# One plain iteration instead of two ahead of the block products of two feed-forward layers

## The chip, the cores and the metric

The kernel runs on one core of a Trainium2 chip. The metric is the device time of one execution in microseconds (us). TensorE (PE in the profile) multiplies, VectorE (DVE) and ScalarE (ACT) work element by element, GpSimd (POOL) helps with normalisation, and SyncE (SP) issues the DMAs. The engines run at the same time, each works through its own instructions strictly in their order, and they wait for each other through semaphores. Before the change the time is 2071.54 us (median of three runs, 2071.41 to 2071.98).

## The reference, cut to what matters

A two-layer encoder over 512 tokens of width 1024, all in float32. Each layer is a SwiGLU feed-forward block, a mixer (neighbourhood attention in layer 0, HGRN2 in layer 1) and a second feed-forward block, each followed by a layer norm.

```python
D_MODEL = 1024; SEQ = 512; DEPTH = 2; D_FF = 2816

def _swiglu(h, w_in, w_out):
    a, b = jnp.split(h @ w_in, 2, axis=-1)
    return (jax.nn.silu(a) * b) @ w_out

for i in range(DEPTH):
    mods = (jax.nn.silu(c) @ ada_w[i] + ada_b[i]).reshape(bsz, 9, D_MODEL)
    h = _modulate(x, mods, 0)
    y = _swiglu(h, ffn_w_in[i, 0], ffn_w_out[i, 0])
    x = _layer_norm(ALPHA * x + 0.5 * mods[:, 2, None, :] * y, ln_g[i, 0], ln_b[i, 0], dtype)
    ...                                   # the mixer, with its own layer norm
    h = _modulate(x, mods, 2)
    y = _swiglu(h, ffn_w_in[i, 1], ffn_w_out[i, 1])
    x = _layer_norm(ALPHA * x + 0.5 * mods[:, 8, None, :] * y, ln_g[i, 2], ln_b[i, 2], dtype)
```

There are four such feed-forward blocks, numbered 0 to 3 here. `h @ w_in` has 22 column tiles of 128 for `a` and 22 for `b`; tile n of `a` and tile n of `b` form pair n.

## The kernel before

**Precision.** Every float32 operand of a matmul is split in two: a rounded high part (`h_hi`, `w_hi`) and the rest (`h_lo`, `w_lo`). A product is three matmuls: high by high, high by low, low by high. ScalarE makes `w_hi` from the loaded weights in `raw`, VectorE makes `w_lo` as `raw - w_hi`. So each weight tile passes SP (DMA), ACT, DVE and PE in this order.

**Phases.** `plan_phases` lists phases, and `drive` writes the instruction order of ACT and DVE for each. A feed-forward block is done in two halves of 12 and 10 pairs; each half has phases that make the gated values `g` and an `out` phase that multiplies by `w_out`. Blocks 0 and 1 make `g` by plain phases (`kind="in"`). Blocks 2 and 3 (`FAST_FFN`) begin half 0 with a plain phase of `PLAIN_ITERS` iterations of two pairs, and do all other pairs in `fast` phases.

**Plain iteration.** Two pairs, four weight tiles of 128x1024 in four slots (s = 0 to 3). TensorE's `unit` (lines 1841 to 1843) does 8 x 3 matmuls of 512 columns for a slot, 96 for two pairs. In the first plain iteration of half 0 `first_units` (lines 1901 to 1918) does 96 such matmuls in another order, while `h` is still being made. After slots 1 and 3, `finish` has ACT take the SiLU (line 819) and DVE multiply and split the result (lines 1179, 1181, 1183: the gate of a pair).

**Block products.** A fast pair computes its two column tiles by seven products of half size in place of eight: each has 4 x 3 matmuls of 256 columns (lines 1855 to 1857), 84 for a pair. They need sums of blocks of `w` and of `h`. DVE makes the sums of `w` for every pair (`fast_sums`, `fast_last_sum`: lines 1077, 1080, 1086). The four sums of `h` are made once for a block, `hs[0..3]` (lines 1148 to 1156, `combine` steps 0 to 3 on DVE); ACT rounds each to `hs_hi` (line 803) and DVE subtracts, giving `hs_lo` (line 1159, `combine` steps 4 to 7). They read `h_full`, which ACT writes at line 984 for these two blocks.

**Order within a fast pair, on TensorE.** Products 0 and 1 need `h` itself; product 1 ends in a bank of its own. Product 2 waits for the second weights, for `hs_lo` of sums 0 and 1, and for `part_kept`: ACT must first copy product 0 out of its PSUM bank (line 766). Product 3 and 4 need the third weights and `hs_lo` 2. Product 5 needs the fourth weights (`fast_low` 3) and `hs_lo` 3. Product 6 needs the last weights and `part_added` 2: DVE must have taken product 4 out of the bank (line 1131). Before a pair starts, the gate of the pair two places earlier must be done (`pair_free`). Meanwhile ACT and DVE prepare the weights of the next pair (`fast` on each engine), so each of these engines has one fixed order of copies, SiLUs, conversions and sums.

**Loads.** SP issues the loads of the weight tiles (line 633) slot by slot, as soon as DVE has made the `w_lo` of what the slot held.

## Time and profile before

| | us |
|---|---|
| median of the runs | 2071.54 (2071.41 to 2071.98) |
| the profiled execution, its own time | 2069.64 |
| its span | 2067.9 |
| TensorE busy | 2039.0 |
| VectorE busy | 1433.9 |
| ScalarE busy | 881.4 |
| GpSimd busy | 244.6 |

In the span, block 2's `g` of half 0 is made from 1007 to 1134 us, and block 3's from 1703 to 1830 us. The rows below are mostly of block 2. A row of a timeline gives the start and the duration in us, the engine, the line and operation, what is written and read, and in brackets the idle time of the engine just before it and what ended it. The distance from one row's start to the next one's is what an instruction costs in a packed queue; the printed duration is some 0.08 us longer, since instructions overlap at their ends.

### The profile page before, as it was taken

To read this page: it belongs to the slowest core of one execution; us is meant where nothing else is said; L and a number is where in the kernel's file an instruction comes from. 1 tells how busy PE (TensorE), PEld (TensorE's weight loads), DVE (VectorE), ACT (ScalarE), POOL (GpSimd) and SP (SyncE) were. 2 spreads that over 40 slices of the span, in tenths; PEclk is the share of its full clock that TensorE was granted. 3 is DMA by queue.
4 is the path that set the end of the run, shared out by engine and by line. 5 is a ranking of instruction groups with operands and counts; after the bars stand their busy time and mean duration, and the time that the engine had idled before them with its cause. 6 is when DMAs were issued, how large, how long until landed. Compare 5 with 4: busy or idle time off the path is not lost.

```text
span 2067.9 us, 34153 instructions
## 1 busy us (share of the span) xinstructions
PE 2039.0 (99%) x11850; PEld 1741.3 (84%) x11850; DVE 1433.9 (69%) x2232; ACT 881.4 (43%) x1420; POOL 244.6 (12%) x236
## 2 busy tenths in 40 slices
PE   7999999999999999999999999999999999999999
PEld 6888888878888888888899899887888878988997
DVE  6867767655558767767788378577767568855875
ACT  5222222455535222222555256375656535533642
POOL 0000000432104000001300000152111232000002
PEclk9999999999999999999999999999999999999999
DMA  9767764342324767664333333332222122333332
GB/s 321 243 181 214 217 193 135 97 112 81 88 82 147 224 182 233 204 177 137 92 92 102 111 92 91 113 112 82 71 71 75 48 72 72 109 99 97 104 94 77
DMA packets 405405, 265.96 MB, mean 129 GB/s; under 512 B 9390, under 2 KB 366158, under 8 KB 405332
## 3 DMA queue, kind: packets, MB, share of 16 engines
q1 hardware_dynamic: 405332, 265.06, 43.3%
q8 instruction: 37, 0.61, 0.1%
q14 instruction: 36, 0.29, 0.0%
HBM read 262.86 MB, written 2.19 MB: 128 GB/s over the span
## 4 chain that ended last, share of the span: by engine, by line
PE 92%; DVE 3%; ACT 2%; POOL 1%; issue 1%; SPq 1%; DMA 0%; DVEq 0%; POOLq 0%; ACTq 0%
PE ps L1841 21%; PE ps L1843 21%; PE ps L1842 21%; PE ps L1855 6%; PE ps L1857 6%; PE ps L1856 6%; PE ps L1937 1%; PE ps L1912 1%; PE ps L1913 1%; PE ps L2193 1%; PE ps L2140 1%; PE ps L1918 1%; PE ps L2125 1%; PE ps L2114 1%; PE ps L2211 1%
## 5 line engine op out<-in xcount | busy, mean ns | idle before, releaser
L812 ACT ACTIVATE w_hi_all<-raw_all 128x1024 fp32r<-128x1024 f32 (+2 forms) x304 | 286.8, 945 | 739.8 <-PE ps L1843 695.3
L1170 DVE TENSOR_TENSOR w_lo_all<-raw_all,w_hi_all 128x1024 fp32r<-128x1024 f32 (+2 forms) x304 | 332.4, 1095 | 353.4 <-ACT w_hi_all L812 352.9
L1841 PE MATMUL ps<-h_hi,w_hi_all 128*128 128x512 f32 x1104 | 434.5, 394 | 2.1 <-ACT gt_sig L913 1.6
L1843 PE MATMUL ps<-h_hi,w_lo_all 128*128 128x512 f32 x1104 | 430.1, 390 | 0.0
L1842 PE MATMUL ps<-h_lo,w_hi_all 128*128 128x512 f32 x1104 | 429.7, 389 | 0.0
L1841 PE MATMUL ps<-g_hi,w_hi_all 128*128 128x512 f32 x704 | 275.0, 391 | 0.0
L1843 PE MATMUL ps<-g_hi,w_lo_all 128*128 128x512 f32 x704 | 274.0, 389 | 0.0
L1842 PE MATMUL ps<-g_lo,w_hi_all 128*128 128x512 f32 x704 | 273.9, 389 | 0.0
L1841 PEld LDWEIGHTS ps<-h_hi,w_hi_all 128*128 128x128 f32 x1104 | 207.2, 188 | 48.7 <-issue 2.3
L1843 PEld LDWEIGHTS ps<-h_hi,w_lo_all 128*128 128x128 f32 x1104 | 207.2, 188 | 43.9
L1842 PEld LDWEIGHTS ps<-h_lo,w_hi_all 128*128 128x128 f32 x1104 | 207.3, 188 | 41.6
L1700 POOL TENSOR_TENSOR zsum<-zsum,x 128x512 f32<-128x512 f32 x42 | 59.6, 1420 | 1382.2 <-DVE x L1207 1381.3
L1855 PE MATMUL ps<-hs_hi,w_hi_all 128*128 128x256 f32 x576 | 163.0, 283 | 0.0
L1856 PE MATMUL ps<-hs_lo,w_hi_all 128*128 128x256 f32 x576 | 163.0, 283 | 0.0
L1857 PE MATMUL ps<-hs_hi,w_lo_all 128*128 128x256 f32 x576 | 163.0, 283 | 0.0
L1843 PEld LDWEIGHTS ps<-g_hi,w_lo_all 128*128 128x128 f32 x704 | 132.1, 188 | 27.7
L1841 PEld LDWEIGHTS ps<-g_hi,w_hi_all 128*128 128x128 f32 x704 | 132.2, 188 | 27.2
L1842 PEld LDWEIGHTS ps<-g_lo,w_hi_all 128*128 128x128 f32 x704 | 132.2, 188 | 26.9
L1440 DVE SCALAR_TENSOR_TENSOR acc<-ada_all,c_silu,acc 128x512 f32<-128x512 f32 x192 | 143.6, 748 | 5.7
L1855 PE MATMUL ps<-h_hi,w_hi_all 128*128 128x256 f32 x432 | 122.4, 283 | 2.5 <-DVE g L1131 2.5
L1857 PE MATMUL ps<-h_hi,w_lo_all 128*128 128x256 f32 x432 | 122.2, 283 | 0.0
L1856 PE MATMUL ps<-h_lo,w_hi_all 128*128 128x256 f32 x432 | 122.2, 283 | 0.0
(318 smaller groups left out, 3455.4 us busy)
## 6 DMA issues: line engine op xcount, KB each, us to landing
raw_all<-in_ffn_w_in_dram SPq DMA_DIRECT2D x176, 512.0 KB, 3.8
ada_all<-in_ada_w_dram SPq DMA_DIRECT2D x128, 512.0 KB, 4.0
raw_all<-in_ffn_w_out_dram SPq DMA_DIRECT2D x64, 384.0 KB, 3.5
raw_all<-in_ffn_w_out_dram SPq DMA_DIRECT2D x64, 320.0 KB, 3.2
raw_all<-in_hgrn_w_in_dram SPq DMA_DIRECT2D x32, 512.0 KB, 3.7
raw_all<-in_na_w_qkv_dram SPq DMA_DIRECT2D x24, 512.0 KB, 3.8
boot<-in_ada_w_dram SPq DMA_DIRECT2D x8, 512.0 KB, 7.1
boot<-in_ada_w_dram SPq DMA_DIRECT2D x16, 256.0 KB, 6.5
```

The lines of the kernel that those rows point to most:

```text
L812: nc.scalar.activation(w_hi[s][:, 0:ph.kt, :], raw[s][:, 0:ph.kt, :], ACT.Copy).then_inc(S.w_hi_done, 1)
L1170: nc.vector.tensor_tensor(w_lo[s][:, 0:ph.kt, :], raw[s][:, 0:ph.kt, :], w_hi[s][:, 0:ph.kt, :].bitcast(F32), ALU.subtract).then_inc(S.w_l ...
L1440: nc.vector.scalar_tensor_tensor(out=acc[:, 0:width], in0=w, scalar=c_silu[:, row:row + 1], in1=acc[:, 0:width], op0=ALU.mult, op1=ALU.add ...
L1700: nc.gpsimd.tensor_tensor(zsum[:], zsum[:], x[:, bass.ds(tile, 1)], ALU.add).then_inc(S.zsum_done, 1)
L1841: nc.tensor.matmul(ps[:, bank, :], w_hi[s][:, k, :], a, start=start and k == 0, stop=False)
L1842: nc.tensor.matmul(ps[:, bank, :], w_hi[s][:, k, :], b, start=False, stop=False)
L1843: ins = nc.tensor.matmul(ps[:, bank, :], w_lo[s][:, k, :], a, start=False, stop=stop and k == ph.kt - 1)
L1855: nc.tensor.matmul(ps[:, bank, 0:TH], w_hi_all[:, at, :], hi[:, k, :], start=start and k == 0, stop=False, skip_group_check=True)
L1856: nc.tensor.matmul(ps[:, bank, 0:TH], w_hi_all[:, at, :], lo[:, k, :], start=False, stop=False, skip_group_check=True)
L1857: ins = nc.tensor.matmul(ps[:, bank, 0:TH], w_lo_all[:, at, :], hi[:, k, :], start=False, stop=k == KH - 1, skip_group_check=True)
L1912: nc.tensor.matmul(ps[:, bank, :], w_hi[s][:, at, :], h_hi[:, at, :], start=at == 0, stop=False)
L1913: nc.tensor.matmul(ps[:, bank, :], w_lo[s][:, at, :], h_hi[:, at, :], start=False, stop=False)
```

## The change

`PLAIN_ITERS` goes from 2 to 1, so in blocks 2 and 3 the plain phase consists of `first_units` alone, and two more pairs per block, 4 in all, are done by block products: 10 in half 0 and 10 in half 1, 20 of 22. The sums of `h` no longer have a second plain iteration to lie in, and `drive` places them anew: sums 0, 1 and 2 right after the layer norm, ahead of the conversion of the first fast pair's weights; `hs_lo` 0 and 1 after the first gate, sum 3 after the third weights, `hs_lo` 2 ahead of the second gate and `hs_lo` 3 behind it. ACT's `hs_hi` copies move with them. The loops of the plain phase that are now empty are left out.

```diff
@@
-PLAIN_ITERS = 2
+PLAIN_ITERS = 1
@@ def steps(i), in drive
                             finish(ph, i - 1, s)
-                        if ph.combine and isinstance(i, int):
-                            combine(ph, s)
@@
-                elif ph.ada is not None and ph.ada.start == 1 or ph.combine:
+                elif ph.ada is not None and ph.ada.start == 1:
                     steps(1)
                     first = 2
@@
+                if ph.combine:
+                    for c in range(3):
+                        combine(ph, c)
                 for s in range(0 if tail is not None and ph.mixer is not None else max(ph.body, 4)):
+                    if ph.combine and s == 3:
+                        combine(ph, 6)
                     if nxt is not None and s < min(nxt.body, 4) and not (ph.last and s == 3):
                         convert(nxt, 0, s)
                     if s < ph.body:
                         finish(ph, ph.iters - 1, s)
-                    if ph.combine:
-                        combine(ph, 4 + s)
+                    if ph.combine and s == 1:
+                        combine(ph, 4)
+                        combine(ph, 5)
+                    if ph.combine and s == 2:
+                        combine(ph, 3)
...
+                if ph.combine:
+                    combine(ph, 7)
                 end(ph, ph.iters - 1)
@@ SyncE: loads
-                else:
+                elif ph.iters > 1:
                     with sp.Fori(1, ph.iters) as i:
@@ ScalarE: combine
-                for c in [(), (0,), (1,), (2,), (3,), (), (), ()][s]:
+                for c in [(0,), (1,), (2,), (3,), (), (), (), ()][s]:
@@ TensorE
-                    if ph.mixer is None:
+                    if ph.mixer is None and ph.iters > 1:
                         with pe.Fori(1 if peeled else 0, ph.iters - 1 if closing else ph.iters) as i:
                             units(i)
```

**VectorE, first place: from the last `h_lo` of block 2's layer norm on.** `hs` are the sums of `h`, `h_all`, `mean` and `w_t` the sums of a fast pair's weights, `g_0` the first gated pair. Before:

```order
L1511 TENSOR_TENSOR h_lo<-h_full,h_hi 128x512 [waits h32_done] x5
L1170 TENSOR_TENSOR w_lo_all<-raw_all,w_hi_all 128x1024 [waits w_hi_done]
L1148 TENSOR_TENSOR hs<-h_full 128x1024 [waits h32_done]
L1170 TENSOR_TENSOR w_lo_all<-raw_all,w_hi_all 128x1024 [waits w_hi_done]
L1179 TENSOR_TENSOR g_0<-s_tmp,ps 128x512 [waits silu_done]
L1181 TENSOR_SCALAR g_hi<-g_0 128x512 [waits pair_free]
L1183 TENSOR_TENSOR g_lo<-g_0,g_hi 128x512 [waits g_hi_done]
L1151 TENSOR_TENSOR hs<-hs,h_full 128x1024 [waits h_summed]
```

After:

```order
L1519 TENSOR_TENSOR h_lo<-h_full,h_hi 128x512 [waits h32_done] x5
L1156 TENSOR_TENSOR hs<-h_full 128x1024 [waits h32_done]
L1159 TENSOR_TENSOR hs<-hs,h_full 128x1024 [waits h_summed]
L1161 TENSOR_TENSOR hs<-h_full 128x1024
L1085 TENSOR_TENSOR h_all<-raw_all 128x1024 [waits w_loaded1,w_loaded0]
L1088 TENSOR_TENSOR mean<-h_all,raw_all 128x512 [waits w_summed]
L1094 TENSOR_TENSOR w_t<-mean,raw_all 128x512 [waits w_summed]
L1103 TENSOR_TENSOR w_lo_all<-raw_all,w_hi_all 128x1024 [waits w_hi_done]
L1103 TENSOR_TENSOR w_lo_all<-mean,w_hi_all 128x512 [waits w_hi_done]
L1187 TENSOR_TENSOR g_0<-s_tmp,ps 128x512 [waits silu_done]
```

Ahead of the first gate there stood two conversions and one sum; now there stand three sums of `h`, three of weights and two conversions.

**VectorE, second place: around the last gate ahead of the first fast pair.** `g_1` is the second gated pair of an iteration; the two conversions at the end are the fourth and fifth weights of the first fast pair, which products 5 and 6 need. Before:

```order
L1159 TENSOR_TENSOR hs_lo<-hs,hs_hi 128x1024 [waits hs_hi_done]
L1095 TENSOR_TENSOR w_lo_all<-h_all,w_hi_all 128x1024 [waits w_hi_done]
L1159 TENSOR_TENSOR hs_lo<-hs,hs_hi 128x1024 [waits hs_hi_done]
L1179 TENSOR_TENSOR g_1<-s_tmp,ps 128x512 [waits silu_done]
L1181 TENSOR_SCALAR g_hi<-g_1 128x512 [waits pair_free]
L1183 TENSOR_TENSOR g_lo<-g_1,g_hi 128x512 [waits g_hi_done]
L1159 TENSOR_TENSOR hs_lo<-hs,hs_hi 128x1024 [waits hs_hi_done]
L1095 TENSOR_TENSOR w_lo_all<-raw_all,w_hi_all 128x512 [waits w_hi_done]
L1095 TENSOR_TENSOR w_lo_all<-w_t,w_hi_all 128x512 [waits w_hi_done]
```

After, from the last part of the first gate on:

```order
L1191 TENSOR_TENSOR g_lo<-g_0,g_hi 128x512 [waits g_hi_done]
L1167 TENSOR_TENSOR hs_lo<-hs,hs_hi 128x1024 [waits hs_hi_done] x2
L1103 TENSOR_TENSOR w_lo_all<-h_all,w_hi_all 128x1024 [waits w_hi_done]
L1164 TENSOR_TENSOR hs<-h_full,hs 128x1024 [waits h_summed]
L1167 TENSOR_TENSOR hs_lo<-hs,hs_hi 128x1024 [waits hs_hi_done]
L1187 TENSOR_TENSOR g_1<-s_tmp,ps 128x512 [waits silu_done]
L1189 TENSOR_SCALAR g_hi<-g_1 128x512 [waits pair_free]
L1191 TENSOR_TENSOR g_lo<-g_1,g_hi 128x512 [waits g_hi_done]
L1167 TENSOR_TENSOR hs_lo<-hs,hs_hi 128x1024 [waits hs_hi_done]
L1103 TENSOR_TENSOR w_lo_all<-raw_all,w_hi_all 128x512 [waits w_hi_done]
L1103 TENSOR_TENSOR w_lo_all<-w_t,w_hi_all 128x512 [waits w_hi_done]
```

The fourth sum of `h` has moved in between the two gates, and with it three of the four `hs_lo`; all of this lies behind the first gate, at which the first fast pair may start.

**ScalarE, around the last `hs_hi`.** `zt` is the copy of a fast pair's product 0 that TensorE's product 2 waits for. Before:

```order
L803 ACTIVATE hs_hi<-hs 128x1024 [waits h_summed]
L756 ACTIVATE w_hi_all<-mean 128x512 [waits unit_done,w_summed]
L819 ACTIVATE s_tmp<-ps 128x512 [waits pair_free,unit_done]
L756 ACTIVATE w_hi_all<-h_all 128x1024 [waits unit_done,w_summed]
L756 ACTIVATE w_hi_all<-raw_all 128x512 [waits unit_done,w_loaded1]
L756 ACTIVATE w_hi_all<-w_t 128x512 [waits unit_done,w_summed]
L819 ACTIVATE s_tmp<-ps 128x512 [waits pair_free,unit_done]
L766 ACTIVATE zt<-ps 128x256 [waits unit_done]
```

After:

```order
L811 ACTIVATE hs_hi<-hs 128x1024 [waits h_summed] x3
L764 ACTIVATE w_hi_all<-raw_all 128x1024 [waits unit_done,w_loaded0]
L764 ACTIVATE w_hi_all<-mean 128x512 [waits unit_done,w_summed]
L827 ACT_TABLE_LOAD [waits pair_free]
L827 ACTIVATE s_tmp<-ps 128x512 [waits unit_done]
L764 ACTIVATE w_hi_all<-h_all 128x1024 [waits unit_done,w_summed]
L764 ACTIVATE w_hi_all<-raw_all 128x512 [waits unit_done,w_loaded1]
L811 ACTIVATE hs_hi<-hs 128x1024 [waits h_summed]
L764 ACTIVATE w_hi_all<-w_t 128x512 [waits unit_done,w_summed]
L827 ACTIVATE s_tmp<-ps 128x512 [waits pair_free,unit_done]
L774 ACTIVATE zt<-ps 128x256 [waits unit_done]
```

The last `hs_hi`, which waits for DVE's fourth sum of `h`, stood seven instructions ahead of the first `zt` copy; now it stands three ahead of it.

## Rows read from the trace of the kernel before

**Rows 1.** The page: busy time of each engine.

```profile
PE 2039.0 (99%) x11850; PEld 1741.3 (84%) x11850; DVE 1433.9 (69%) x2232; ACT 881.4 (43%) x1420; POOL 244.6 (12%) x236
```

**Rows 2.** Stretches: length; busy us of PE, PEld, DVE, ACT, POOL; granted clock, DMA, GB/s.

```profile
1030.10:1051.99 21.89, 21.89 (x96) 18.13 (x97) 19.11 (x22) 9.39 (x12) 0.00 (x0) 1.00 0.34 97
1051.99:1063.52 11.53, 10.29 (x86) 10.12 (x84) 10.02 (x14) 5.74 (x10) 0.00 (x0) 1.00 0.21 58
1063.52:1134.10 70.58, 70.58 (x591) 70.58 (x590) 59.93 (x90) 42.22 (x76) 0.00 (x0) 1.00 0.35 101
```

**Rows 3.** Timeline of TensorE: second plain iteration's start, product 6, the next pair.

```profile
1030.10 0.50 PE L1841 MATMUL ps<-h_hi,w_hi_all 128*128 128x512 f32 x1 [0.22 <-DVE g L1179]
...
1062.02 0.36 PE L1855 MATMUL ps<-h_hi,w_hi_all 128*128 128x256 f32 x1 [1.24 <-DVE g L1131]
...
1063.52 0.28 PE L1855 MATMUL ps<-h_hi,w_hi_all 128*128 128x256 f32 x1
```

**Rows 4.** Timeline of VectorE, from the last h_lo to the first fast pair.

```profile
1020.78 1.00 DVE L1511 TENSOR_TENSOR h_lo<-h_full,h_hi 128x512 fp32r<-128x512 f32 x1
...
1025.63 1.23 DVE L1170 TENSOR_TENSOR w_lo_all<-raw_all,w_hi_all 128x1024 fp32r<-128x1024 f32 x1 [3.85 <-ACT w_hi_all L812]
...
1029.36 0.69 DVE L1179 TENSOR_TENSOR g<-s_tmp,ps 128x512 f32<-128x512 f32 x1 [0.23 <-ACT s_tmp L819]
...
1031.15 1.22 DVE L1151 TENSOR_TENSOR hs<-hs,h_full 128x1024 f32<-128x1024 f32 x1
1032.29 1.22 DVE L1170 TENSOR_TENSOR w_lo_all<-raw_all,w_hi_all 128x1024 fp32r<-128x1024 f32 x1
...
1038.62 1.22 DVE L1077 TENSOR_TENSOR h_all<-raw_all 128x1024 f32<-128x1024 f32 x1
1039.87 0.69 DVE L1080 TENSOR_TENSOR mean<-h_all,raw_all 128x512 f32<-128x512 f32 x1
1040.60 0.69 DVE L1086 TENSOR_TENSOR w_t<-mean,raw_all 128x512 f32<-128x512 f32 x1
...
1059.39 0.42 DVE L1123 TENSOR_TENSOR s_tmp<-ps,zt 128x256 f32<-128x256 f32 x1
1059.72 0.68 DVE L1086 TENSOR_TENSOR w_t<-mean,raw_all 128x512 f32<-128x512 f32 x1
1060.32 1.22 DVE L1095 TENSOR_TENSOR w_lo_all<-raw_all,w_hi_all 128x1024 fp32r<-128x1024 f32 x1
1061.46 0.41 DVE L1131 TENSOR_TENSOR g<-sq,ps 128x256 f32<-128x256 f32 x1
```

**Rows 5.** Timeline of ScalarE in the same time.

```profile
1027.43 1.28 ACT L819 ACT_TABLE_LOAD   x1
1028.73 0.60 ACT L819 ACTIVATE s_tmp<-ps 128x512 f32<-128x512 f32 x1
1029.22 1.05 ACT L803 ACTIVATE hs_hi<-hs 128x1024 fp32r<-128x1024 f32 x1
1030.17 1.05 ACT L812 ACTIVATE w_hi_all<-raw_all 128x1024 fp32r<-128x1024 f32 x1
...
1041.37 0.63 ACT L756 ACTIVATE w_hi_all<-mean 128x512 fp32r<-128x512 f32 x1 [1.57 <-DVE w_t L1086]
1041.91 0.58 ACT L819 ACTIVATE s_tmp<-ps 128x512 f32<-128x512 f32 x1
...
1053.62 0.38 ACT L766 ACTIVATE zt<-ps 128x256 f32<-128x256 f32 x1 [0.26 <-PE ps L1857]
```

**Rows 6.** Timelines of VectorE and GpSimd during block 2's layer norm.

```profile
1010.78 2.16 DVE L1170 TENSOR_TENSOR w_lo_all<-raw_all,w_hi_all 128x1024 fp32r<-128x1024 f32 x1
...
1022.42 0.76 POOL L1685 TENSOR_SCALAR x<-x,AG,AB 128x512 f32<-128x512 f32 x1
```

**Rows 7.** The weight loads of line 633 from 1005 to 1060 us.

```profile
DMA to landing us min/median/max: 3.6/3.7/4.3
```

**Rows 8.** The last stretch of the span, columns as in rows 2.

```profile
2066.00:2067.90 1.90, 0.00 (x0) 0.00 (x0) 0.00 (x0) 0.00 (x0) 0.00 (x0) 0.50 0.53 205
```

## The prediction

> **What bounds the kernel now.** I read the page first: TensorE is busy for 99% of the span, VectorE for 69% [rows 1]. So time can be saved only by taking matmuls away, and lost only where TensorE is made to wait. Then the stretches of block 2 [rows 2]: the second plain iteration (two pairs, 96 matmuls) takes 21.89 us, the first fast pair 11.53 us, and the seven fast pairs behind it 70.56 us (1063.52 to 1134.08), 10.08 us each. The timeline of TensorE [rows 3] says why the first is longer: product 6 waits 1.24 us for VectorE's line 1131. In the steady fast pairs VectorE is busy 59.93/7 = 8.6 us of 10.08, so it keeps up, but with only 1.5 us to spare. In the second plain iteration it is already busy for 19.11 of 21.89 us. The reader is to see that VectorE had little room just where the change takes time away from it. Block 3 has the same picture, some 696 us later; I take both as equal.
>
> **What is removed and added on TensorE.** Per block one plain iteration of 21.75 us (21.89 less 0.14 of first-matmul latency [rows 2]) goes and two fast pairs of 10.08 us come: 1.6 us saved, 3.2 us for both blocks, if nothing waits. To this comes the 1.24 us wait per block, if it goes, and 0.3 us of first-matmul latencies. As a balance: before, half 0's last fast pair ends at 1134.1. After the change it ends at 1030.1 + 10 x 10.08 + S = 1130.9 + S, where S is all the waiting that falls on the first fast pair. The kernel gains if S is below 3.2 us per block and loses if S is above.
>
> **What S is: VectorE's queue.** Costs per instruction, as distances of starts [rows 4]: 1024-wide 1.14 us (1031.15 to 1032.29), or 1.25 when the next one needs its result (1038.62 to 1039.87); 512-wide 0.73 with such a dependence and 0.60 without; 256-wide 0.33; a gate's three instructions 1.79 (1029.36 to 1031.15). ScalarE [rows 5]: 0.95 for 1024-wide, 0.54 for 512-wide, 0.49 for a SiLU, 1.30 for the table load, 0.38 for a zt copy. A handoff costs 0.04 us between these two, and 0.05 to 0.15 to TensorE (1061.87 to 1062.02 [rows 3, 4]).
> VectorE is free of the last h_lo at 1021.7 [rows 4]. Its order after the change, walked through:
> - Sum 0 of h from 1021.7. GpSimd still scales x until 1023.2 [rows 6], and a 1024-wide conversion beside such work took 2.16 us in place of 1.22. That bounds the extra between 0 and 0.94; I take 0.4, since GpSimd has only 1.5 us left. So sums 1 and 2 start at 1023.4 and 1024.5, the three sums of weights at 1025.6, 1026.9 and 1027.6, the first two conversions at 1028.2 and 1029.4. VectorE's idle time of old (up to 1025.6) does cover three sums of h, but the sums of weights, 2.6 us, come in front of the gate too.
> - ScalarE: third hs_hi at 1025.8, two conversions, the table load at 1028.2, SiLU 1029.5 to 1030.1. The gate starts at 1030.15, its first part is done at 1030.85, and TensorE starts the first fast pair at 1030.9: 0.8 us late.
> - VectorE: gate to 1031.9, hs_lo 0 and 1 to 1034.2, third weights to 1035.3, sum 3 of h done at 1036.6, then hs_lo 2 to 1037.6.
> - **The new wait.** ScalarE's fourth hs_hi waits for sum 3, from about 1031.5 on. Behind it stand the fifth weights, the second SiLU and the zt copy of product 0. TensorE has finished products 0 and 1 at 1030.9 + 24 x 0.12 = 1033.8 and needs that copy for product 2. ScalarE: hs_hi 3 at 1036.6, weights 1037.6, SiLU 1038.1, copy 1038.6 to 1039.0. Product 2 starts at 1039.1: a wait of 5.3 us. It does not depend on the h sums themselves: hs_lo 0 and 1 are there at 1034.3.
> - VectorE's second gate waits for that SiLU, until 1038.7. Then gate to 1040.5, hs_lo 3 to 1041.7, fourth and fifth weights to 1042.9, next pair's two sums to 1044.7, line 1123's addition to 1045.1, third sum to 1045.7, first weights of the next pair to 1046.8, line 1131's subtraction done at 1047.25. Product 6 may start at 1047.4.
> - TensorE: products 2 to 5 take 4 x 1.44 us, 1039.1 to 1044.9, then it waits 2.5 us for line 1131. Product 6 runs 1047.4 to 1048.9, taking 1.5 us as from 1062.02 to 1063.52 [rows 3].
> So the first fast pair ends at 1048.9 and S = 1048.9 - 1030.1 - 10.1 = 8.7 us (0.8 + 5.3 + 2.5, and roundings).
>
> **What comes next.** Nothing waits again: VectorE reaches line 1131 of the second pair some 2.4 + 6.3 us after the first (in packed order this subtraction and three more instructions, then nine of the second pair: five of 0.60, three of 1.14 to 1.25, one of 0.33), at 1055.5; product 4 of that pair, which it needs, ends at 1056.3, so it is done by 1056.7, and product 6 is due at 1048.9 + 8.6 = 1057.5. With 1.5 us of slack per pair the lag is gone in the next. The half ends at 1030.1 + 100.8 + 8.7 = 1139.6 in place of 1134.1: 5.5 us later per block, 11.1 us for both (with 5.55 unrounded). Loads: SP issues four loads of weights for two block pairs where it issued four for the plain iteration; the last slot's old weights are converted at 1012.9 [rows 6], and a load lands 3.6 to 4.3 us after issue [rows 7], so the raw weights are there by about 1017, long before 1025.6. They cost nothing. The out phases, half 1, the mixers and GpSimd's work are not touched; the two pairs that move keep the same number of gates.
>
> **TensorE's clock.** The granted clock is 1.00, the level of 2.4 GHz, all through blocks 2 and 3 [rows 2]; it is 0.50, 1.2 GHz, in the last 1.9 us of the span, when TensorE has no more work [rows 8]. A wait of 5.3 us in mid-kernel is as long as nothing in the trace of block 2 or 3. At half clock a 256-column matmul cannot keep 0.12 us; taken as twice that, products 2 to 5 would end at 1039.1 + 11.5 = 1050.6 at worst, against the 1047.4 at which product 6 may start anyway. The first 2.5 us of such a loss are hidden behind the wait for line 1131.
> The Trainium skill, page "TensorE: Matmul & The Clock Gate", section on the clock gate, says that the throttled state is the default and that activity releases it, so that an idle stretch costs twice, once as a wait and again as slow matmuls. By that rule this change would lose more than the waits; rows 8 agree that idleness brings the clock down, and show no price for it.
>
> **The rivals.**
> - *VectorE alone sets the end.* If the zt copy got through early, the second gate would not wait for its SiLU (1.1 us less) and product 6 could start at 1046.3. S = 7.6, 8.9 us in all: 2080.4. Against it: the order on ScalarE puts hs_hi 3 ahead, and its queue is strictly in order.
> - *The clock falls and costs.* Product 6 at 1050.6 in place of 1047.4 per block: 6.4 us more, 2089.0; half of it if the clock comes back during these products, 2085.8. For it: rows 8. Against it: the slack of 2.5 us.
> - *The sums hide.* VectorE would have to reach line 1131 in time for product 6, at 1030.1 + 8.6. It would take 8.6 us less work in its queue than I count (1047.25 against 1038.7). If so, S is 0 and 3.2 us per block are gained: 2071.5 - 6.4 = 2065.1, faster. This decides at S = 3.2 us. For it: VectorE idles 3.85 us ahead of 1025.63 [rows 4], which is what the three early sums are put into. Against it: the walk uses these microseconds already.
> - *S near 3.2 us*, waits and saved matmuls in balance: 2071.5, the same.
>
> **How the numbers follow.** The profiled execution took 2069.64 us; with 11.1 us more it would be 2080.7. The median is 1.9 us above it, so I forecast 2071.54 + 11.1 = 2082.6. My own case has 0.74, its range from 2081.0 to 2085.0: GpSimd's share of the first sum, 0 to 0.94 us in place of 0.4, moves it by -0.8 or +1.1 us, and handoffs of 0.1 us in a chain of some 25 by another 1. VectorE alone 0.07, clock 0.09, hidden 0.05, balance 0.05. The range that should hold the time 8 times in 10 is 2079.5 to 2087.0, which takes in the first rival and the milder clock case. A measurement can tell about 0.2% (4.1 us) from no change. Slower by more than that 0.90, within it 0.05, faster 0.05.
>
> **What would show it right or wrong.** In the profile after: ten fast pairs in half 0 of each block; a wait of about 5 us of line 1863 (the old 1855) at product 2, ended by ScalarE's zt copy, and about 2.5 us at product 6, ended by VectorE's line 1139; ScalarE idle some 5 us ahead of the fourth hs_hi, released by sum 3; no wait at later pairs; the second pair's start 18.8 us after 1030.1. The step most likely to be wrong is the wait at product 2. If products 2 to 5 stand further apart than 0.12 us per matmul, or the granted clock is below 1.00 there, the clock took part. If the table load or the first SiLU comes earlier, S shrinks by as much.

## The result, and the profile after

The changed kernel takes 2081.71 us (median of four runs, 2081.03 to 2085.22), against 2071.47 us (four runs, 2069.67 to 2071.98) for the kernel before on the same chip: a ratio of 1.0056, 95% interval 1.0041 to 1.0071. It is slower by 10.2 us in the medians. The profiled executions took 2081.03 and 2069.64 us, 11.4 us apart. The prediction was 2082.6 us with a range of 2079.5 to 2087.0, and 90% for slower by more than 0.2%.

The page, as in [rows 1]: TensorE's busy time is the same within 0.4 us although 4 pairs changed their kind, and the share has gone from 99% to 98%. VectorE and ScalarE are busy 20.8 and 14.5 us longer.

```profile
PE 2039.4 (98%) x11994; PEld 1749.0 (84%) x11994; DVE 1454.7 (70%) x2264; ACT 895.9 (43%) x1452; POOL 252.4 (12%) x236
```

That TensorE's busy time did not fall by the saved matmuls is told by the stretches of time, with the columns of [rows 2]:

```profile
1030.10:1049.00 18.90, 13.00 (x85) 12.63 (x86) 17.59 (x23) 8.24 (x14) 0.00 (x0) 0.82 0.22 65
1037.50:1044.30 6.80, 5.22 (x24) 5.22 (x25) 5.71 (x9) 2.86 (x6) 0.00 (x0) 0.50 0.08 24
1740.60:1744.00 3.40, 3.14 (x14) 3.14 (x15) 3.33 (x5) 1.33 (x3) 0.00 (x0) 0.50 0.00 0
1049.00:1139.60 90.60, 90.60 (x757) 90.60 (x756) 77.67 (x116) 54.56 (x98) 0.00 (x0) 1.00 0.35 102
```

The first fast pair now takes 18.9 us from where it could have started, and TensorE stands idle for 5.9 of them. In a part of it, in block 2 and in block 3, the granted clock is 0.50 (1.2 GHz in place of 2.4). The nine fast pairs behind it run without a gap, 90.6/9 = 10.07 us each, at full clock: the whole loss lies in the first.

What TensorE waited for, from the list of waits (total us, times, longest):

```profile
PE ps L1863 <- ACT zt L774: 9.9, 2, 5.0
...
PE ps L1863 <- DVE g L1187: 2.7, 2, 1.4
...
PE ps L1863 <- DVE g L1139: 0.9, 1, 0.9
```

The wait for ScalarE's `zt` copy, 5.0 us in each block, is the new one. The first gate (line 1187) is waited for twice 1.4 us, where the second plain iteration of before waited 0.22 us [rows 3]. Line 1139, the old 1131, is waited for once, not twice.

The timeline of TensorE shows the places. Block 2 first, then the waits in block 3:

```profile
1030.99 0.39 PE L1863 MATMUL ps<-h_hi,w_hi_all 128*128 128x256 f32 x1 [1.36 <-DVE g L1187]
...
1039.08 0.58 PE L1863 MATMUL ps<-hs_hi,w_hi_all 128*128 128x256 f32 x1 [4.97 <-ACT zt L774]
1039.46 0.41 PE L1864 MATMUL ps<-hs_lo,w_hi_all 128*128 128x256 f32 x1
1039.68 0.41 PE L1865 MATMUL ps<-hs_hi,w_lo_all 128*128 128x256 f32 x1
...
1044.34 0.28 PE L1863 MATMUL ps<-hs_hi,w_hi_all 128*128 128x256 f32 x1
1044.46 0.28 PE L1864 MATMUL ps<-hs_lo,w_hi_all 128*128 128x256 f32 x1
...
1047.41 0.36 PE L1863 MATMUL ps<-h_hi,w_hi_all 128*128 128x256 f32 x1
```

```profile
1740.86 0.58 PE L1863 MATMUL ps<-hs_hi,w_hi_all 128*128 128x256 f32 x1 [4.97 <-ACT zt L774]
...
1749.19 0.35 PE L1863 MATMUL ps<-h_hi,w_hi_all 128*128 128x256 f32 x1 [0.94 <-DVE g L1139]
```

Product 0 starts at 1030.99, product 2 at 1039.08, product 6 at 1047.41. Behind the wait the matmuls of products 2 and 3 stand 0.21 us apart, at half clock, and from 1044.3 on 0.12 us. In block 2 they thereby end just when product 6 may start, and there is no wait left to see; in block 3 the slow part is half as long and 0.94 us of wait remain. The end is the same in both blocks, for VectorE's line 1139 sets it.

ScalarE in the same time; this answers to [rows 5] and is the heart of the matter:

```profile
1036.70 1.06 ACT L811 ACTIVATE hs_hi<-hs 128x1024 fp32r<-128x1024 f32 x1 [5.01 <-DVE hs L1164]
1037.66 0.61 ACT L764 ACTIVATE w_hi_all<-w_t 128x512 fp32r<-128x512 f32 x1
1038.18 0.58 ACT L827 ACTIVATE s_tmp<-ps 128x512 f32<-128x512 f32 x1
1038.66 0.37 ACT L774 ACTIVATE zt<-ps 128x256 f32<-128x256 f32 x1
```

ScalarE stands idle for 5.01 us ahead of the fourth `hs_hi`, though the `zt` copy three places behind it could have been made by 1034. VectorE, as in [rows 4]:

```profile
1022.75 1.60 DVE L1159 TENSOR_TENSOR hs<-hs,h_full 128x1024 f32<-128x1024 f32 x1
...
1026.65 0.98 DVE L1088 TENSOR_TENSOR mean<-h_all,raw_all 128x512 f32<-128x512 f32 x1
...
1035.44 1.22 DVE L1164 TENSOR_TENSOR hs<-h_full,hs 128x1024 f32<-128x1024 f32 x1
...
1038.79 0.69 DVE L1187 TENSOR_TENSOR g<-s_tmp,ps 128x512 f32<-128x512 f32 x1 [0.99 <-ACT s_tmp L827]
...
1046.85 0.42 DVE L1139 TENSOR_TENSOR g<-sq,ps 128x256 f32<-128x256 f32 x1
...
1056.33 0.42 DVE L1139 TENSOR_TENSOR g<-sq,ps 128x256 f32<-128x256 f32 x1 [0.65 <-PE ps L1865]
```

Between 1021.51 and 1046.85 VectorE is idle only for 0.99 us ahead of the second gate and for a few tenths elsewhere: the walked queue. In the second pair (last row) it is VectorE that waits, so the lag is made up.

**A measure for the experiments.** Whole times hold things that have nothing to do with the change, so I also measured one stretch in each profile: from the first multiplication by `h_lo` in `first_units` (1022.5 before, 1022.2 after) to the start of the last high-by-high matmul of half 0's last fast pair (1133.7 and 1139.3). All lengths in us:

| kernel | block 2 | block 3 | the 585 us between them |
|---|---|---|---|
| before | 111.2 | 111.3 | 584.7 |
| after | 117.1 | 117.0 | 584.7 |
| `a_block2` | 117.0 | 111.3 | 586.7 |
| `a_zt` | 118.7 | 117.4 | 586.6 |
| `a_busy` | 117.0 | 117.1 | 587.0 |
| `a_vplus` | 119.7 | 119.7 | 586.4 |
| `a_pool` | 119.0 | 120.4 | 586.6 |
| `a_zt_busy` | 115.9 | 115.9 | 585.1 |
| `b_hl3` | 110.1 | 110.1 | 586.4 |
| `b_early` | 109.8 | 109.8 | 585.2 |

The last column is work that no experiment touches. Where it is above 586, the profile has a stretch at granted clock 0.50 somewhere between 1398 and 1414 us, behind a wait of TensorE for `gt_sig` in the mixer (1.6 us before and after, 1.9 to 2.0 in all the others, `a_zt_busy` and `b_early` too, which have no such stretch). The clock fell there in some executions and not in others; what decides it stays open. It is some 2 us of noise in every whole time below, and may be part of why the medians differ by 10.2 us where the profiles differ by 11.4.

### The profile page after: what moved, and what is told of

Read it like the earlier page. It is cut to its first block, busy times and chain, and to the rows that moved or that the text cites. A ratio compares the mean times of both kernels' runs of the same rounds, so it can differ in the third digit from the quotient of the medians.

```text
span 2079.3 us, 34709 instructions
## 1 busy us (share of the span) xinstructions
PE 2039.4 (98%) x11994; PEld 1749.0 (84%) x11994; DVE 1454.7 (70%) x2264; ACT 895.9 (43%) x1452; POOL 252.4 (12%) x236
## 4 chain that ended last, share of the span: by engine, by line
PE 90%; DVE 4%; ACT 3%; POOL 1%; issue 1%; SPq 1%; DMA 0%; DVEq 0%; ACTq 0%; POOLq 0%
PE ps L1849 20%; PE ps L1851 20%; PE ps L1850 20%; PE ps L1863 6%; PE ps L1864 6%; PE ps L1865 6%; PE ps L1920 1%; PE ps L1921 1%; PE ps L1945 1%; PE ps L1926 1%; PE ps L2201 1%; PE ps L2148 1%; PE ps L2133 1%; PE ps L2122 1%; PE ps L2219 1%
## 5 line engine op out<-in xcount | busy, mean ns | idle before, releaser
L1849 PE MATMUL ps<-h_hi,w_hi_all 128*128 128x512 f32 x1040 | 409.3, 394 | 1.6 <-ACT gt_sig L921 1.6
L1851 PE MATMUL ps<-h_hi,w_lo_all 128*128 128x512 f32 x1040 | 405.2, 390 | 0.0
L1850 PE MATMUL ps<-h_lo,w_hi_all 128*128 128x512 f32 x1040 | 404.8, 389 | 0.0
L1849 PEld LDWEIGHTS ps<-h_hi,w_hi_all 128*128 128x128 f32 x1040 | 195.2, 188 | 45.2 <-issue 2.3
L1863 PE MATMUL ps<-hs_hi,w_hi_all 128*128 128x256 f32 x640 | 183.2, 286 | 9.9 <-ACT zt L774 9.9
L1864 PE MATMUL ps<-hs_lo,w_hi_all 128*128 128x256 f32 x640 | 182.8, 286 | 0.0
L1865 PE MATMUL ps<-hs_hi,w_lo_all 128*128 128x256 f32 x640 | 182.6, 285 | 0.0
L1863 PE MATMUL ps<-h_hi,w_hi_all 128*128 128x256 f32 x480 | 136.2, 284 | 3.7 <-DVE g L1187 2.7
L1864 PE MATMUL ps<-h_lo,w_hi_all 128*128 128x256 f32 x480 | 135.8, 283 | 0.0
L1865 PE MATMUL ps<-h_hi,w_lo_all 128*128 128x256 f32 x480 | 135.8, 283 | 0.0
```

The costliest lines, as they stand in the source:

```text
L1849: nc.tensor.matmul(ps[:, bank, :], w_hi[s][:, k, :], a, start=start and k == 0, stop=False)
L1850: nc.tensor.matmul(ps[:, bank, :], w_hi[s][:, k, :], b, start=False, stop=False)
L1851: ins = nc.tensor.matmul(ps[:, bank, :], w_lo[s][:, k, :], a, start=False, stop=stop and k == ph.kt - 1)
L1863: nc.tensor.matmul(ps[:, bank, 0:TH], w_hi_all[:, at, :], hi[:, k, :], start=start and k == 0, stop=False, skip_group_check=True)
L1864: nc.tensor.matmul(ps[:, bank, 0:TH], w_hi_all[:, at, :], lo[:, k, :], start=False, stop=False, skip_group_check=True)
L1865: ins = nc.tensor.matmul(ps[:, bank, 0:TH], w_lo_all[:, at, :], hi[:, k, :], start=False, stop=k == KH - 1, skip_group_check=True)
```

## Experiments

My theory: the first fast pair ends when two queues let it. ScalarE's order holds product 2 back (the fourth `hs_hi` stands ahead of the `zt` copy), and VectorE's queue, with the sums now in it, holds product 6 back. The rivals: ScalarE's order alone is the cause; the clock that falls during the wait is the cause; TensorE's wait for the first gate or another place outside the pair.

### One block at a time

`a_block2` makes the change in block 2 alone; block 3 stays as before. The new placements then hang on `ph.iters == 1`, of which one is shown.

```diff
-PLAIN_ITERS = 1
+PLAIN_ITERS = {2: 1, 3: 2}
...
-            plain = pairs // 2 if ffn not in FAST_FFN else PLAIN_ITERS if half == 0 else 0
+            plain = pairs // 2 if ffn not in FAST_FFN else PLAIN_ITERS[ffn] if half == 0 else 0
...
-                if ph.combine:
+                if ph.combine and ph.iters == 1:
                     for c in range(3):
```

> The change in block 2 alone; block 3 keeps its two plain iterations and the old places of the sums. The theory (all of the loss is waiting that falls on the first fast pair of each block) expects half of the change's loss: half 0 of block 2 as in the changed kernel, that of block 3 as before, 2071.5 + 5.1 = 2076.6 us. Rival: the loss comes from elsewhere, from the code that the longer loops or the missing loop move, or once for the kernel: then it is either all there (2081.6) or gone (2071.5).

Measured: 2077.35 us (six runs, 2075.35 to 2078.41) against 2071.01 (eleven runs of before on this chip), ratio 1.0031 (1.0019 to 1.0043). The stretch of block 2 is 117.0 us as in the changed kernel, that of block 3 111.3 us as before. So block 2 adds its 5.8 us by itself, block 3 is not touched by it, and the loss lies within the stretch. The wait for the first gate, a rival, is too short to be the loss: product 0 starts at 1030.99, 0.9 us behind the 1030.1 of before, and the pair takes 8.8 us more than a steady one (18.9 less 10.07). The whole time is 0.75 us above what was expected, with the 2 us of the last column in it.

### ScalarE's order alone

`a_zt` moves ScalarE's fourth `hs_hi` behind the first pair's `zt` copy. All else is the changed kernel.

```diff
@@ ScalarE: fast
                 keep(kept_1[par], x_bank, 1)
+                if ph.half == 0 and first_of(i) and par == 0:
+                    act.wait_ge(S.h_summed, ph.c0)
+                    nc.scalar.activation(hs_hi[:, 3], hs[:, 3], ACT.Copy).then_inc(S.hs_hi_done, 1)
@@ ScalarE: combine
-                for c in [(0,), (1,), (2,), (3,), (), (), (), ()][s]:
+                for c in [(0,), (1,), (2,), (), (), (), (), ()][s]:
```

> The changed kernel with ScalarE's fourth hs_hi moved behind the first fast pair's first zt copy, so that the copy waits for nothing of VectorE. Theory (VectorE's queue sets the end, the wait at product 2 mostly replaces a longer wait at product 6): the wait at product 2 falls from 5.0 to about 0.6 us and comes back at products 4 to 6; only the 1.0 us is gained for which VectorE's second gate waited for the SiLU, 1.1 us per block, so 2081.6 - 2.2 = 2079.4 us. Rival (the wait at product 2 is a loss of its own): 5.0 us per block come back, 2071.6 us.

Measured: 2085.32 us (four runs, 2084.7 to 2085.91), ratio 1.0071 (1.0055 to 1.0086). That is 3.6 us slower than the changed kernel, where 2 us less were expected: a miss in the sign. The two stretches are longer by 1.6 and 0.4 us, and 1.9 us lie between them, in the part that no experiment touches. By whole times alone the two kernels' intervals overlap; the stretches show the miss. TensorE, VectorE and ScalarE in its trace, and a stretch of it:

```profile
1031.92 0.38 PE L1866 MATMUL ps<-h_hi,w_hi_all 128*128 128x256 f32 x1 [1.38 <-DVE g L1190]
...
1035.47 0.36 PE L1866 MATMUL ps<-hs_hi,w_hi_all 128*128 128x256 f32 x1 [0.43 <-DVE hs_lo L1170]
...
1039.96 0.39 PE L1866 MATMUL ps<-hs_hi,w_hi_all 128*128 128x256 f32 x1 [1.38 <-ACT zt L774]
...
1042.49 0.35 PE L1866 MATMUL ps<-hs_hi,w_hi_all 128*128 128x256 f32 x1 [0.84 <-DVE w_lo_all L1106]
...
1047.26 0.55 PE L1866 MATMUL ps<-h_hi,w_hi_all 128*128 128x256 f32 x1 [3.11 <-DVE g L1142]
```

```profile
1033.64 0.39 ACT L774 ACTIVATE zt<-ps 128x256 f32<-128x256 f32 x1
1037.63 1.06 ACT L779 ACTIVATE hs_hi<-hs 128x1024 fp32r<-128x1024 f32 x1 [3.60 <-DVE hs L1167]
...
1039.54 0.36 ACT L774 ACTIVATE zt<-ps 128x256 f32<-128x256 f32 x1
```

```profile
1046.70 0.41 DVE L1142 TENSOR_TENSOR g<-sq,ps 128x256 f32<-128x256 f32 x1
```

```profile
1046.49:1053.32 6.83, 6.06 (x28) 6.09 (x29) 5.97 (x10) 2.13 (x6) 0.00 (x0) 0.50 0.53 154
```

The copy is made at 1033.64, and the wait at product 2 shrinks from 4.97 to 0.43 us. The same idle time turns up further on (1.38 us at product 4, 0.84 at product 5) and most of it at product 6, 3.11 us. At product 4 it is ScalarE once more: the pair's second `zt` copy, at 1039.54, now stands behind the fourth `hs_hi`, which waits for VectorE's sum as before. VectorE's subtraction, line 1142, starts 14.78 us after product 0 (1046.70 less 1031.92), against 15.86 us in the changed kernel (1046.85 less 1030.99). These 1.08 us are the gain that I had expected, within 0.1 us. But the clock falls at 1046.49, late in the new wait, and now nothing is late behind product 6: 6.06 us of matmuls run at half clock. At 0.214 us a matmul in place of 0.12 (22 steps from 1039.46 to 1044.16, and those behind) 44% of such time is lost, by this estimate 2.7 us here. In the changed kernel the slow matmuls were those of products 2 and 3, ahead of a wait that took the loss in. Net this makes 1.6 us more in block 2; measured, 118.7 less 117.1, 1.6 us. In block 3 the slow part is 3.4 us long, 1.5 lost against 1.1 gained: 117.4 against 117.0.

So ScalarE's order is not the cause of most of the loss: without it, it is 1.1 us per block less at equal clock. And the clock, hidden before, costs as soon as it falls in a place without cover.

### The clock alone

`a_busy` keeps TensorE at work during the long wait: 20 matmuls of 512 columns between products 1 and 2, into a bank that nobody reads at that time. The first two pairs are written out ahead of the loop for it. The result of these matmuls is not used.

```diff
+BUSY = 20
...
-            def fast(ph, i, par):
+            def fast(ph, i, par, busy=0):
...
                 product(1, y_bank, *quarter(0, 1), True)
+                for _ in range(busy):
+                    nc.tensor.matmul(ps[:, 4, :], h_hi[:, 0, 0:P], h_hi[:, 0, :], start=True, stop=True)
```

> The changed kernel with 20 matmuls of 512 columns more between products 1 and 2 of the first fast pair of each block (4.5 us of the 5.0 us that TensorE waits there), into a PSUM bank that nobody reads, so that TensorE is never idle for more than about a microsecond; the first two fast pairs are written out ahead of the loop for it. Theory (the slow clock in this place is hidden, since product 6 waits for VectorE anyway): granted clock 1.00 throughout, products 2 to 5 at 0.12 us per matmul, the wait at product 6 back to 2.5 us, time unchanged at 2081.5 us within 1 us. Rival (the clock costs time): faster, by 1 to 3 us, and without the changed kernel's slowest executions (2085.2 us was one of four).

Measured: 2084.05 us (five runs, 2083.3 to 2084.32), ratio 1.0065 (1.0051 to 1.0079). The clock stays up through the pair, and the wait at product 6 is back:

```profile
1030.10:1049.00 18.90, 15.08 (x104) 13.82 (x105) 17.59 (x23) 8.19 (x14) 0.00 (x0) 1.00 0.22 64
```

```profile
1047.58 0.36 PE L1864 MATMUL ps<-h_hi,w_hi_all 128*128 128x256 f32 x1 [2.30 <-DVE g L1140]
```

It is 2.30 us, and the stretches are 117.0 and 117.1 us as without the filling. This settles that the half clock of the changed kernel costs nothing: it only took the place of the wait that I had forecast as 2.5 us. In block 2 this was close: 24 matmuls at 0.094 us more each are 2.26 us, of the 2.30 us that were there. The whole time is 2.3 us above the changed kernel's and 2.5 above what was expected. The profile has it outside the two blocks (587.0 in place of 584.7 between them), where the clock fell once near 1405 us:

```profile
1404.00:1408.00 4.00, 3.17 (x8) 2.49 (x9) 2.24 (x4) 2.69 (x5) 3.14 (x3) 0.63 0.45 131
```

All five runs lie above 2083, and of the changed kernel's four only one. From one profile it can't be said that the fall near 1405 accounts for all of them. The mean granted clock is 0.999 in the two shortest (2083.30 and 2083.48 us) and 0.998 in the other three (2084.05 to 2084.32 us).

### VectorE's queue, made longer

`a_vplus` adds two subtractions of 512 columns ahead of `hs_lo` 3, with their results unused. If VectorE's queue sets the end, their 1.2 us must appear in full.

```diff
@@ VectorE: combine
+                    if c == 3:
+                        for b in range(2):
+                            nc.vector.tensor_tensor(ps[:, 4 + b, :].rearrange("p (k t) -> p k t", k=2), hs[:, 3, 2 * b:2 * b + 2],
+                                                    hs_hi[:, 3, 2 * b:2 * b + 2].bitcast(F32), ALU.subtract)
                     nc.vector.tensor_tensor(hs_lo[:, c], hs[:, c], hs_hi[:, c].bitcast(F32), ALU.subtract).then_inc(S.hs_ready, 1)
```

> The changed kernel with two 512-wide subtractions more on VectorE just ahead of hs_lo 3 of each block, results into PSUM banks that nobody reads: 1.2 us more in VectorE's queue ahead of line 1139. Theory (VectorE's queue sets when product 6 may start): 1.2 us later per block, 2081.6 + 2.4 = 2084.0 us. Rival (ScalarE or the weights set it, VectorE has room): 2081.6 us.

Measured: 2087.18 us (four runs, 2084.84 to 2088.71), ratio 1.0077 (1.0061 to 1.0092), and both stretches 119.7 us: 2.6 us more, where 1.2 were put in.

```profile
1049.26 0.36 PE L1867 MATMUL ps<-h_hi,w_hi_all 128*128 128x256 f32 x1 [2.14 <-DVE g L1139]
```

```profile
1049.72:1053.13 3.41, 3.41 (x19) 3.41 (x18) 2.96 (x5) 0.90 (x2) 0.00 (x0) 0.50 0.55 158
```

From product 2 (1039.73) to product 6 it is 9.53 us, against 8.33 in the changed kernel: exactly the 1.2 us of the two instructions. The other 1.4 us come from a second fall of the clock right behind the wait of 2.14 us at product 6, where there is nothing left to hide it (44% of 3.41 us is 1.5, an estimate as above). The rival, that some VectorE work is hidden, falls; the size was missed for want of the clock.

### Both causes away

After these runs a sum could be made: without ScalarE's wait 1.1 us less per block, and with the clock kept up nothing to pay for it. `a_zt_busy` is `a_zt` with 6 filling matmuls behind product 3 and 12 behind product 5, and the first two pairs written out ahead of the loop as in `a_busy`.

```diff
@@ TensorE: fast, against a_zt
+                def fill(times):
+                    for _ in range(times):
+                        nc.tensor.matmul(ps[:, 4, :], h_hi[:, 0, 0:P], h_hi[:, 0, :], start=True, stop=True)
...
                 product(3, z_bank, *summed(0), True)
+                fill(busy[0])
...
                 product(5, z_bank, *summed(3), False)
+                fill(busy[1])
```

> The kernel of the run in which ScalarE's zt copy comes ahead of its fourth hs_hi, with 6 matmuls of 512 columns more behind product 3 and 12 more behind product 5 of the first fast pair of each block (1.4 and 2.7 us, inside the waits of 1.4 and 3.1 us there), so that TensorE is not idle long enough for its clock to fall. That run took 118.7 and 117.4 us from the last part of first_units to the end of half 0's fast pairs, in blocks 2 and 3, where 116.0 were expected; its clock was at 0.50 for some microseconds behind product 6. Theory (the surplus is slow matmuls, the wait at product 2 was worth only 1.1 us): granted clock 1.00 in both stretches, 116.0 us in each, 2079.5 us; with the slow stretch in the mixer that the last runs showed, up to 2081.5 us. Rival (the surplus comes from the order on ScalarE itself, copies that now come late): 118 us again in both blocks, 2085 us.

Measured: 2080.11 us (five runs, 2079.61 to 2081.72) against 2070.15 (nine runs) on its chip, ratio 1.0049 (1.0035 to 1.0063); 5.2 us less than `a_zt`, or 4.3 when each is taken against its own runs of before. The stretches are 115.9 us in both blocks, with 116.0 expected.

```profile
1030.10:1049.00 18.90, 15.93 (x109) 14.12 (x109) 18.58 (x25) 8.88 (x17) 0.00 (x0) 1.00 0.26 74
1700.00:1830.00 130.00, 126.41 (x935) 119.44 (x934) 117.72 (x168) 78.47 (x132) 19.59 (x14) 1.00 0.31 90
```

The clock is 1.00 in both blocks, and VectorE is busy for 18.58 of the 18.90 us of the first pair (the sum of its idle times there was 1.3 us in the changed kernel). With this the surplus of `a_zt` is shown to be the clock. What is left of the loss, 115.9 less 111.2 = 4.7 us per block, stands with the wait at product 2 gone and the clock up. VectorE stands idle for only 0.3 us in this pair, and `a_vplus` shows that work added to its queue comes out in full at product 6: what is left is VectorE's queue. No run took work off that queue in the changed kernel with success (the next one tried), so the 4.7 us are not shown by removal.

### VectorE's work given to GpSimd

If VectorE's queue is the bound, work taken off it should help. `a_pool` is `a_zt` with sums 2 and 3 of `h` and `hs_lo` 2 and 3 made by GpSimd; ScalarE's third `hs_hi` moves behind the first SiLU.

```diff
@@ VectorE: combine, against a_zt
-                if s == 2:
-                    nc.vector.tensor_tensor(hs[:, 2], a11, a21, ALU.subtract).then_inc(S.h_summed, 1)
-                if s == 3:
-                    dve.wait_ge(S.h_summed, ph.c0 + 2)
-                    nc.vector.tensor_tensor(hs[:, 3], a12, hs[:, 1], ALU.add).then_inc(S.h_summed, 1)
-                for c in [(), (), (), (), (0,), (1,), (2,), (3,)][s]:
+                for c in [(), (), (), (), (0,), (1,), (), ()][s]:
@@ ScalarE: combine
-                for c in [(0,), (1,), (2,), (), (), (), (), ()][s]:
+                for c in [(0,), (1,), (), (), (2,), (), (), ()][s]:
@@ GpSimd
+            def pool_sums(ph):
...
+                nc.gpsimd.tensor_tensor(hs[:, 2], a11, a21, ALU.subtract).then_inc(S.h_summed, 1)
+                pool.wait_ge(S.h_summed, ph.c0 + 3)
+                nc.gpsimd.tensor_tensor(hs[:, 3], a12, hs[:, 1], ALU.add).then_inc(S.h_summed, 1)
+                for c in (2, 3):
+                    pool.wait_ge(S.hs_ready, ph.c0 + c)
+                    pool.wait_ge(S.hs_hi_done, ph.c0 + c + 1)
+                    nc.gpsimd.tensor_tensor(hs_lo[:, c], hs[:, c], hs_hi[:, c].bitcast(F32), ALU.subtract).then_inc(S.hs_ready, 1)
```

> a_zt, and sums 2 and 3 of h and hs_lo 2 and 3 are made by GpSimd, which is idle from 1024 us on: 4.56 us less in VectorE's queue per block. If the two engines ran independently of each other, the waiting of the first fast pair would be about 3.1 us, the same as the 3.2 us that the two saved plain pairs give back: 2071.3 us. If they slow each other down as the 2.16 us conversion beside GpSimd's work in the layer norm (against 1.22 us) says, VectorE loses 0.9 us for each instruction that runs beside GpSimd's 10 to 14 us of work, nearly all that it is relieved of: 2078 us. I expect a value between, 2075 us.

Measured: 2090.91 us (four runs, 2090.19 to 2092.2), ratio 1.0093 (1.0077 to 1.0109): the slowest of all, outside of what either theory expected. Against `a_zt`'s profiled execution, 3.1 us of it lie ahead of block 2 (the first `h_lo` multiplication is at 1026.2 in place of 1023.1; the clock fell once near 42 us, which explains a part, and the rest stays open), and 0.3 and 3.0 us in the two stretches. The timeline of both engines says what happened in the pair:

```profile
1029.97 2.81 POOL L1802 TENSOR_TENSOR hs<-h_full 128x1024 f32<-128x1024 f32 x1
1030.57 2.77 DVE L1097 TENSOR_TENSOR w_t<-mean,raw_all 128x512 f32<-128x512 f32 x1
...
1032.86 2.68 POOL L1804 TENSOR_TENSOR hs<-h_full,hs 128x1024 f32<-128x1024 f32 x1
1033.26 3.37 DVE L1106 TENSOR_TENSOR w_lo_all<-raw_all,w_hi_all 128x1024 fp32r<-128x1024 f32 x1
...
1041.37 5.85 POOL L1808 TENSOR_TENSOR hs_lo<-hs,hs_hi 128x1024 fp32r<-128x1024 f32 x2 [5.82 <-DVE hs_lo L1165]
1042.34 0.68 DVE L1185 TENSOR_TENSOR g<-s_tmp,ps 128x512 f32<-128x512 f32 x1
1043.06 1.92 DVE L1187 TENSOR_SCALAR g_hi<-g 128x512 fp32r<-128x512 f32 x1
1045.01 2.75 DVE L1189 TENSOR_TENSOR g_lo<-g,g_hi 128x512 fp32r<-128x512 f32 x1
```

The sum `w_t` takes 2.77 us in place of 0.69 [rows 4], the conversion 3.37 in place of 1.22, `g_hi` 1.92 in place of 0.43, `g_lo` 2.75 in place of 0.69. They do not seem to run slower but to stand still: `w_t` ends at 1033.34, 0.56 us behind the end of GpSimd's sum (1032.78), the conversion at 1036.63, 1.09 us behind the end of the next (1035.54), and `g_lo` at 1047.76, 0.54 us behind the end of GpSimd's last (1047.22), each about its own undisturbed length. The gate's first part, which reads one operand from PSUM, passes beside GpSimd in 0.68 us. GpSimd needs 2.7 to 2.9 us for what VectorE does in 1.14, and VectorE is stopped for most of it: the four rows add up to 7.8 us of standing, where 4.56 us of work were taken away. So the handing over costs VectorE more than doing it. The theory that VectorE's queue is the bound is neither refuted nor borne out by this miss. TensorE waits 4.31 us for the first gate, in place of 1.38, because VectorE was stopped; the SiLU that this gate needs was done at 1033.11, 4 us ahead of the gate, so ScalarE's new order is not the reason.

### The same two steps in the kernel before

The wait of 1.24 us at product 6 in the kernel before [rows 3] is the same kind of lateness. `b_hl3` puts `hs_lo` 3 ahead of the last gate, into the 3.13 us for which VectorE waits there in the kernel before; `b_early` also moves the fourth weights of the first fast pair ahead of that gate.

```profile
1053.40 0.69 DVE L1179 TENSOR_TENSOR g<-s_tmp,ps 128x512 f32<-128x512 f32 x1 [3.13 <-ACT s_tmp L819]
```

```diff
@@ drive, b_hl3 against before
                         convert(nxt, 0, s)
+                    if ph.combine and s == 3:
+                        combine(ph, 7)
                     if s < ph.body:
                         finish(ph, ph.iters - 1, s)
-                    if ph.combine:
+                    if ph.combine and s < 3:
                         combine(ph, 4 + s)
@@ VectorE, b_early against b_hl3
-                fast_low(ph, i, par, 3)
+                if later or ph.half == 1:
+                    fast_low(ph, i, par, 3)
...
-                    for c in [(0,), (1,), (2,), ()][s]:
+                    for c in [(0,), (1,), (2,), (3,) if ph.half == 0 else ()][s]:
```

> The kernel before with one edit: hs_lo 3 is made ahead of the last gate of the second plain iteration, in the 3.1 us for which VectorE waits there for the SiLU, instead of behind it. Theory (VectorE's queue sets when product 6 of the first fast pair may start, here too): line 1131 comes 1.14 us earlier and the wait of 1.24 us at product 6 falls to about 0.2 us; 1.05 us per block gained, 2071.5 - 2.1 = 2069.4 us. Rival (product 6 is bound by product 4 or by ScalarE's copies): 2071.5 us.

> As b_hl3, and the first fast pair's fourth weights (512 wide, 0.60 us) are converted ahead of that gate too. Theory: VectorE reaches line 1131 0.6 us earlier again, and the rest of the wait goes, until product 4's end binds: 1.24 us per block gained, 2071.5 - 2.5 = 2069.0 us. Rival: 2071.5 us.

Measured, with twenty runs of before at 2071.01 us: `b_hl3` 2068.81 us (eleven runs, 2067.06 to 2069.77), ratio 0.9988 (0.9978 to 0.9997); `b_early` 2067.51 us (eleven runs, 2066.48 to 2071.1), ratio 0.9984 (0.9975 to 0.9994). The stretches are 110.1 and 109.8 us, against 111.2. VectorE's subtraction that product 6 needs starts at 1061.46 before [rows 4]. Product 6 and this subtraction in `b_hl3`, then in `b_early`:

```profile
1061.63 0.35 PE L1857 MATMUL ps<-h_hi,w_hi_all 128*128 128x256 f32 x1
```

```profile
1061.07 0.41 DVE L1133 TENSOR_TENSOR g<-sq,ps 128x256 f32<-128x256 f32 x1
```

```profile
1060.86 0.28 PE L1858 MATMUL ps<-h_hi,w_hi_all 128*128 128x256 f32 x1
```

```profile
1059.96 0.41 DVE L1134 TENSOR_TENSOR g<-sq,ps 128x256 f32<-128x256 f32 x1
```

Block 2 does not begin at the same time in the three traces, so I count from the stretch's start (1022.5, 1023.2, 1022.7): the subtraction comes 39.0 us behind it before, 37.9 in `b_hl3` and 37.3 in `b_early`, 1.1 and 1.7 us earlier, as the work that was moved (1.14 and 0.60 us) says. Product 6 starts 1.52 us behind the matmul ahead of it before, 0.39 us in `b_hl3` and 0.12 us, the spacing in a packed queue, in `b_early`. So `b_hl3` leaves some 0.3 us of wait, too little for the list of waits, and takes 1.1 us off the stretch; the second step takes this rest, and then it is no longer VectorE that binds. The intervals of the two overlap, so that the second step helps the whole time is not shown. Both beat both kernels, `b_early` the changed one by 14 us. They show from the other side that the work on VectorE between the last gate and line 1131 is what the first fast pair waits for. Part of this work is not even for the pair that waits: the changed kernel's VectorE makes two sums, the third sum and the first conversion of the next pair between 1042.92 and 1046.85, 3.6 us that stand ahead of line 1139. Whether they could go behind it at a gain no run tests.

## Why the prediction was right, point by point

**The balance.** Nine pairs at 10.07 us behind the first, no wait among them, the half's last product ending at 1139.6: as walked. Since the result hangs on S alone, the question is whether S was right for the right reasons.

**Product 0.** Forecast 1030.9, came 1030.99 in a run in which `h_lo` was ready 0.2 us earlier. So this part was 0.3 us dearer than I had it. The step that was mis-sized is the extra for GpSimd's company. I took 0.4 us on sum 0; it fell on sum 1, whose step to the next start is 1.52 us in place of 1.14, and on `mean`, 1.02 in place of 0.73 [rows 4]: 0.67 us together. GpSimd was not done at 1023.2, as I had it, but at 1027.1 (last section), so both instructions ran beside it.

**The new wait at product 2.** Forecast: fourth `hs_hi` at 1036.6, copy at 1038.6, product 2 at 1039.1, 5.3 us of wait. Came: 1036.70, 1038.66, 1039.08, and 4.97 us; I had let the twenty-fourth matmul end where the next would have started, 0.3 us early. This was the step I called most likely to be wrong, and it held.

**The second gate and product 6.** Forecast: gate 1038.7, line 1139 done at 1047.25, product 6 at 1047.4. Came: 1038.79, start at 1046.85 and product 6 at 1047.41. The forecast wait of 2.5 us is seen in `a_busy` as 2.30 us; in the changed kernel half clock filled it.

**The next pair.** Forecast: line 1139 done by 1056.7, in time. It starts at 1056.33 behind a wait for TensorE. Right.

**The clock.** I gave 0.09 to "the clock falls and costs". It did fall, and it did not cost. That it would fall I had not forecast, only how much could be hidden if it did: the 2.5 us of slack. `a_busy` bears this out. That the slow stretch ended within the slack, 2.26 of 2.30 us in block 2, was luck as far as the prediction goes: nothing in it said how long the stretch would last. The Trainium skill, page "TensorE: Matmul & The Clock Gate", section "HAM oscillation — how this bites in real kernels", has a wait after which the matmuls start at the lower clock, and counts the time that they take longer as a penalty on top of the wait. The traces of `a_zt` and `a_vplus` agree, with 2.7 and 1.4 us; in the changed kernel the matmuls were slow too, but the end came no later, because a wait on another engine stood behind them.

**The rivals.** "VectorE alone sets the end" gave 2080.4 us. That is 8.9 us above before, 4.4 per block. The kernel that makes this case, `a_zt_busy`, is 4.7 us per block longer than before, which is 4.4 and the 0.3 of product 0; its whole time, 2080.11 us, was taken on another chip and is 10.0 us above before there. Its difference of 1.1 us per block to the changed kernel is also the whole worth of the `zt` wait, although that wait is 5.0 us long in the list of waits: of these 5.0 us, 3.9 would have been waited for at products 2 to 6 anyway. "The sums hide" needed VectorE 8.6 us earlier and was never near. The balance point, S of 3.2 us, was not reached by any version of the changed kernel.

**The sizes.** The stretches are 5.9 and 5.7 us longer where 5.5 were forecast, which fits the 0.3 us of product 0. On the span's own clock block 2's half ends at 1139.6 as forecast, since its layer norm was done 0.2 us earlier. The profiled executions are 11.4 us apart, where 11.1 were forecast. The median of the four runs is 0.9 us under the forecast, within their spread.

What stays open: what decides whether the clock falls near 1405 us, and with it up to 2 us of each whole time; why `a_busy`, whose two stretches equal the changed kernel's, was above 2083 us in all of its runs; and what sets the length of a slow stretch.

## What to carry to other kernels

When work is taken from the engine that sets the end, the new end is found by walking the other engines' queues instruction by instruction, with the distances of starts from a trace; sums of busy shares would have shown VectorE at 70% and missed it. In such a walk ask what stands ahead of every copy that frees a buffer for the bounding engine, and what a listed wait is worth once the next wait behind it is counted: here 1.1 of 5.0 us. A wait that is made shorter or moved can bring TensorE's slow stretch to a place with nothing behind it to hide it, so look at the granted clock on both sides before calling a removed wait a gain.
